# Two feed-forward products with the two parts of x side by side: one 512-column product for two of 256

## What is computed

```python
def swiglu(x, wg, wu, wd):
    return (jax.nn.silu(x @ wg) * (x @ wu)) @ wd
...
        m = jnp.einsum('bsd,df->bsf', rms_norm_2(h, mlp_norm[l]), w_mlp_in[l])
        m = jnp.square(jax.nn.relu(m))
        h = h + jnp.einsum('bsf,fd->bsd', m, w_mlp_out[l])
```

## Time and profile before

| | us |
|---|---|
| median of 3 runs | 2073.51 |
| lowest, highest | 2073.36, 2076.2 |
| the profiled execution | 2071.93 |
| its span, first to last instruction | 2069.9 |
| mean granted clock of TensorE, share of full speed | 0.976 |

### The profile page before, as it was taken

One profiled execution on the slowest core, in us unless ns is written; L12 is line 12 of the kernel. 1 busy time (PEld: TensorE's weight loads), 2 busy tenths in 40 slices (PEclk: granted clock), 3 DMA queues, 4 the chain that ended last, 5 costly groups with the idle time before them and its releaser, 6 DMA issues.

```text
span 2069.9 us, 33025 instructions
## 1 busy us (share of the span) xinstructions
PE 1932.9 (93%) x13818; PEld 1758.2 (85%) x13818; DVE 1147.3 (55%) x1219; ACT 383.9 (19%) x718; POOL 601.3 (29%) x505
## 2 busy tenths in 40 slices
PE   4899999999997878899989999889999999889999
PEld 2576777887997867799989997789999999689999
DVE  3652221325258976644575776675556676576554
ACT  1200000113122230211122122411112102432110
POOL 0111111121235611233333332133334333123333
PEclk8899999999999989999999999999999999999999
DMA  8336655321233212355544443235554434134552
GB/s 311 113 108 218 237 210 201 131 102 61 103 127 128 95 69 102 112 188 183 181 152 166 143 143 122 102 126 184 182 183 175 151 140 156 69 141 165 183 183 102
DMA packets 44913, 307.83 MB, mean 149 GB/s; under 512 B 5376, under 2 KB 5888, under 8 KB 8320
## 3 DMA queue, kind: packets, MB, share of 16 engines
q1 hardware_dynamic: 40752, 292.66, 39.8%
q10 hardware_dynamic: 4048, 13.49, 1.8%
HBM read 302.98 MB, written 3.15 MB: 148 GB/s over the span
## 4 chain that ended last, share of the span: by engine, by line
PE 78%; DVE 12%; issue 4%; POOL 2%; ACT 2%; DMA 2%; ACTq 0%; DVEq 0%; POOLq 0%
PE ps L1830 23%; PE ps L1831 22%; PE ps L1832 22%; DVE wlo L643 3%; POOL whi L570 2%; DMA ws<-in_hyc 2%; PE ps L1956 1%; PE ps L2312 1%; PE ps L1925 1%; PE ps L2219 1%; PE ps L2336 1%; DVE xlo L703 1%; PE ps L1987 1%; PE ps L2179 1%; PE ps L2289 1%
## 5 line engine op out<-in xcount | busy, mean ns | idle before, releaser
L1830 PE MATMUL ps<-xhi,whi 128*128 128x256 f32 (+1 forms) x3680 | 1121.0, 305 | 37.5 <-DVE xlo L651 21.4
L1831 PE MATMUL ps<-xlo,whi 128*128 128x256 f32 (+1 forms) x3680 | 1104.1, 300 | 0.0
L1832 PE MATMUL ps<-xhi,wlo 128*128 128x256 f32 (+1 forms) x3680 | 1103.6, 300 | 0.0
L643 DVE TENSOR_TENSOR wlo<-landing,whi 128x2048 fp32r<-128x2048 f32 x242 | 562.3, 2323 | 460.0 <-POOL whi L570 459.3
L1830 PEld LDWEIGHTS ps<-xhi,whi 128*128 128x128 f32 x3680 | 710.1, 193 | 74.2 <-issue 31.1
L1831 PEld LDWEIGHTS ps<-xlo,whi 128*128 128x128 f32 x3680 | 710.3, 193 | 22.8 <-issue 2.2
L1832 PEld LDWEIGHTS ps<-xhi,wlo 128*128 128x128 f32 x3680 | 709.6, 193 | 21.2
L569 POOL TENSOR_TENSOR whi<-landing,ones 128x128 fp32r<-128x128 f32 x242 | 124.4, 514 | 1445.1 <-PE ps L1832 1404.2
L570 POOL TENSOR_SCALAR whi<-landing 128x1920 fp32r<-128x1920 f32 x242 | 442.9, 1830 | 0.0
L881 DVE TENSOR_TENSOR big<-big,ps 128x512 f32<-128x512 f32 x22 | 15.1, 687 | 184.7 <-ACT big L1555 184.7
L1467 ACT ACTIVATE xhi<-big 128x512 fp32r (+3 forms) x66 | 45.9, 696 | 385.7 <-PE ps L1832 331.2
(11 more groups left out here) (269 smaller groups left out, 1379.3 us busy)
## 6 DMA issues: line engine op xcount, KB each, us to landing
landing<-in_stream SPq DMA_DIRECT2D x250, 1024.0 KB, 4.8
ws<-in_stream SPq DMA_DIRECT2D x28, 1024.0 KB, 4.8
spectra<-big ACTq DMA_DIRECT2D x8, 256.0 KB, 6.1
ws<-spectra ACTq DMA_DIRECT2D x2, 1024.0 KB, 4.9
ws<-in_tabs ACTq DMA_DIRECT2D x1, 1280.0 KB, 5.5
h<-in_xT ACTq DMA_DIRECT2D x1, 1024.0 KB, 15.7
ws<-in_window ACTq DMA_DIRECT2D x1, 1024.0 KB, 23.7
ws<-in_ctxT ACTq DMA_DIRECT2D x1, 1024.0 KB, 28.2
```

Of the source, the lines that this page charges most:

```text
L643: v.tensor_tensor(wlo[:, s % 2], landing[:, s], whi[:, s % 2].bitcast(F32), ALU.subtract).then_inc(lo_done, 1)
L1830: mm(out, w_hi, x_hi, start=first, stop=False, skip_group_check=True)
L1831: mm(out, w_hi, x_lo, start=False, stop=False, skip_group_check=True)
L1832: return mm(out, w_lo, x_hi, start=False, stop=last, skip_group_check=True)
```

## The change

The low part of x goes beside its high part: into columns 256 to 511 of `xhi` instead of `xlo` (lines 681 and 703 of before). A wide product of 512 columns, high weights by both parts, takes the place of two of 256; the product of low weights and high x stays. The bank of a column block then holds in its left half high by high plus low weights by high x, and in its right half high weights by low x. Each panel takes two banks in both stages, so MLP-in has two pairs in turn (banks 0 to 3) where it had four banks.

The halves are summed when the banks are read: ACT copies the right halves into `low_sums` (new, in place of value tiles not needed then), DVE adds them to the left halves into `rtmp`. Silu and the multiplication, or relu and square, work on `rtmp`. PE waits for `pair_read`, which DVE's sum raises, before it writes a pair again. In MLP-in a turn of DVE's loop is now: `low` of panel i+5, sum (`whole`) and relu of panel i+3.

```diff
-        rtmp = [W(tmpA, 2 * T), W(tmpA + 512, 2 * T)]
+        rtmp = [W(tmpA, 2, T), W(tmpA + 512, 2, T)]
+        low_sums = [W(NTABS, 2, T), W(NTABS + 512, 2, T)]
...
+        low_copied, pair_read = lsem("low_copied", N_MIN), lsem("pair_read", N_MIN)
...
-                    lo = xlo[:, j, dst0:dst0 + T]
+                    lo = xhi[:, j, T:2 * T] if n == 4 else xlo[:, j, dst0:dst0 + T]
...
-                        v.scalar_tensor_tensor(xlo[:, k, 0:T], h[:, k], gain(k), xhi[:, k, 0:T].bitcast(F32), ALU.mult,
+                        lo = xhi[:, k, T:2 * T] if j % 2 else xlo[:, k, 0:T]
+                        v.scalar_tensor_tensor(lo, h[:, k], gain(k), xhi[:, k, 0:T].bitcast(F32), ALU.mult,
...
+            def up2_stage():
                 def body(i, g, s):
                     low(g + 1, (s + 1) % SLOTS)
                     if isinstance(i, int) and i == N_UP - 1:
-                        r0 = (R_DOWN1, R_DOWN2)[which]
-                        part_low(hid_src(t)(0), r0, r0, t)
-                    dve.wait_ge(silu_done, which * KFF + i + 1)
-                    hid = hid_chunk(i, t)
-                    bank = 2 * ((s - g0) % UNROLL) + 1
-                    v.tensor_tensor(hid, hid, ps[:, bank, 0:t], ALU.mult).then_inc(hid_done, 1)
-                panel_loop(dve, g0, N_UP, body)
+                        part_low(hid_src(T)(0), R_DOWN2, R_DOWN2, T)
+                    bank = 2 * ((s - G_UP2) % UNROLL)
+                    both = rtmp[(s - G_UP2) % 2]
+                    dve.wait_ge(low_copied, i + 1)
+                    v.tensor_tensor(both, ps[:, bank:bank + 2, 0:T], low_sums[(s - G_UP2) % 2], ALU.add).then_inc(pair_read, 1)
+                    dve.wait_ge(silu_done, KFF + i + 1)
+                    hid = hid_chunk(i, T)
+                    v.tensor_tensor(hid, hid, both[:, 1], ALU.mult).then_inc(hid_done, 1)
+                panel_loop(dve, G_UP2, N_UP, body)
...
-                def relu(i, j):
-                    dve.wait_ge(panel_used, first[0] + 1 + i)
+                def whole(i, j):
+                    dve.wait_ge(low_copied, at(low_copied, l, 1, base=N_UP) + i)
                     if not isinstance(i, int) or i >= 2:
                         dve.wait_ge(m_done, at(m_done, l, -1) + i)
-                    v.scalar_tensor_tensor(rtmp[j % 2].rearrange("p (c t) -> p c t", t=T),
-                                           ps[:, j].rearrange("p (c t) -> p c t", t=T), 0.0,
-                                           rstd[:, 1].unsqueeze(1).to_broadcast([P, 2, T]), ALU.max, ALU.mult
-                                           ).then_inc(relu_done, 1)
+                    bank = 2 * (j % 2)
+                    v.tensor_tensor(rtmp[j % 2], ps[:, bank:bank + 2, 0:T], low_sums[j % 2], ALU.add).then_inc(pair_read, 1)
+                def relu(i, j):
+                    dve.wait_ge(pair_read, at(pair_read, l, 1, base=N_UP) + i)
+                    v.scalar_tensor_tensor(rtmp[j % 2], rtmp[j % 2], 0.0, rstd[:, 1].unsqueeze(1).to_broadcast([P, 2, T]),
+                                           ALU.max, ALU.mult).then_inc(relu_done, 1)
                 def low_min(i):
                     low(first[0] + i, (first[1] + i) % SLOTS)
                 low_min(1)
                 fold(2 * l + 1)
                 low_min(2)
+                whole(0, 0)
                 dve.wait_ge(inv_done, 2 * l + 2)
                 relu(0, 0)
-                low_min(3)
-                relu(1, 1)
-                relu(2, 2)
-                low_min(4)
+                for i in (1, 2):
+                    low_min(i + 2)
+                    whole(i, i)
+                    relu(i, i)
                 def relu_low(i, g, s):
-                    relu(i + 3, (s - first[1] + 3) % UNROLL)
+                    j = (s - first[1] + 3) % UNROLL
                     low(g + 5, (s + 5) % SLOTS)
+                    whole(i + 3, j)
+                    relu(i + 3, j)
                 panel_loop(dve, layer_panel(l, O_MIN), N_MIN - UNROLL, relu_low)
                 part_low(chunk_src(0)(0), rl + RO_MOUT, R_LAYER + RO_MOUT, T)
+                whole(N_MIN - 1, (N_MIN - 1) % UNROLL)
                 relu(N_MIN - 1, (N_MIN - 1) % UNROLL)
...
+            def up2_stage():
                 def body(i, g, s):
                     if isinstance(i, int) and i == N_UP - 1:
-                        act.wait_ge(hid_done, which * KFF + ROWK)
-                        first_high(hid_src(t), (R_DOWN1, R_DOWN2)[which], t, which + 1)
+                        act.wait_ge(hid_done, KFF + ROWK)
+                        first_high(hid_src(T), R_DOWN2, T, 2)
+                    bank = 2 * ((s - G_UP2) % UNROLL)
                     act.wait_ge(panel_used, g + 1)
-                    a.activation(hid_chunk(i, t), ps[:, 2 * ((s - g0) % UNROLL), 0:t], ACT.Silu).then_inc(silu_done, 1)
-                panel_loop(act, g0, N_UP, body)
+                    if not isinstance(i, int) or i >= 2:
+                        act.wait_ge(pair_read, i - 1)
+                    a.activation(low_sums[(s - G_UP2) % 2], ps[:, bank:bank + 2, T:2 * T], ACT.Identity).then_inc(low_copied, 1)
+                    act.wait_ge(pair_read, i + 1)
+                    a.activation(hid_chunk(i, T), rtmp[(s - G_UP2) % 2][:, 0], ACT.Silu).then_inc(silu_done, 1)
+                for i in range(UNROLL):
+                    body(i, G_UP2 + i, (G_UP2 + i) % UNROLL)
+                panel_loop(act, G_UP2 + UNROLL, N_UP - UNROLL, lambda i, g, s: body(i + UNROLL, g, s))
...
-                boundary_rms(2 * l + 1, step)
                 mfirst = layer_panel(l, O_MIN)
-                def square(i, g, s):
+                def copy_low(i, g, j):
+                    act.wait_ge(panel_used, g + 1)
+                    if not isinstance(i, int) or i >= 2:
+                        act.wait_ge(pair_read, at(pair_read, l, -1, base=N_UP) + i)
+                    bank = 2 * (j % 2)
+                    a.activation(low_sums[j % 2], ps[:, bank:bank + 2, T:2 * T], ACT.Identity).then_inc(low_copied, 1)
+                def square(i, j):
+                    act.wait_ge(relu_done, at(relu_done, l, 1) + i)
+                    a.activation(big[:, ds(i * 2, 2), :], rtmp[j % 2], ACT.Square).then_inc(m_done, 1)
+                for i in range(UNROLL):
+                    copy_low(i, mfirst[0] + i, i)
+                    if i == 0:
+                        boundary_rms(2 * l + 1, step)
+                    square(i, i)
+                def copy_square(i, g, s):
                     j = (s - mfirst[1]) % UNROLL
-                    act.wait_ge(relu_done, at(relu_done, l, 1) + i)
-                    a.activation(big[:, ds(i * 2, 2), :].rearrange("p c t -> p (c t)"), rtmp[j % 2], ACT.Square
-                                 ).then_inc(m_done, 1)
-                panel_loop(act, mfirst, N_MIN - UNROLL, square)
+                    copy_low(i + UNROLL, g, j)
+                    square(i + UNROLL, j)
+                panel_loop(act, layer_panel(l, O_MIN + UNROLL), N_MIN - 2 * UNROLL, copy_square)
                 for i in range(N_MIN - UNROLL, N_MIN):
                     if i == N_MIN - 1:
                         act.wait_ge(m_done, at(m_done, l, 1))
                         first_high(chunk_src(0), R_LAYER + RO_MOUT, T, at(x_free, l, 1, base=2))
-                    square(i, layer_panel(l, O_MIN + i)[0], (mfirst[1] + i) % UNROLL)
+                    copy_low(i, layer_panel(l, O_MIN + i)[0], i % UNROLL)
+                    square(i, i % UNROLL)
...
+            def wide_product(out, s, k, c, first, last):
+                w = slice(k * COLS + c * P, k * COLS + (c + 1) * P)
+                mm(out, whi[:, s % 2, w], xhi[:, k], start=first, stop=False, skip_group_check=True)
+                return mm(out[:, 0:T], wlo[:, s % 2, w], xhi[:, k, 0:T], start=False, stop=last, skip_group_check=True)
+            def wide_panel(s, bank):
+                for c in range(2):
+                    for k in range(KD):
+                        last = wide_product(ps[:, bank + c], s, k, c, k == 0, k == KD - 1)
+                return last
+            def wide_streamed(s, bank, base, order):
+                for n, k in enumerate(order):
+                    pe.wait_ge(norm_lo, base + (n + 1))
+                    for c in range(2):
+                        last = wide_product(ps[:, bank + c], s, k, c, n == 0, n == KD - 1)
+                return last
+            def wide_last(s, bank):
+                for k in range(KD):
+                    for c in range(2):
+                        last = wide_product(ps[:, bank + c], s, k, c, k == 0, k == KD - 1)
+                    if k == KD // 2 - 1:
+                        last.then_inc(x_free, 1)
                 return last
...
+            def up2_stage():
                 def one(i, g, s, reused):
-                    j = (s - g0) % UNROLL
+                    bank = 2 * ((s - G_UP2) % UNROLL)
                     pe.wait_ge(lo_done, g - (N_LEAD - 1))
```

(27 more changed lines are left out.)

10 lines of the change are left out of this document (4 added, 6 removed).

## The result

Five executions of the changed kernel took 2083.34 to 2086.72 us, median **2085.94**; five of the kernel before beside them 2072.7 to 2076.2, median 2073.51. The ratio is **1.0057** (95% interval 1.0042 to 1.0071): 12.4 us slower, where 5.7 were forecast. The profiled execution took 2086.65 us, its span 2084.9. Repeated on another chip, the same two kernels gave 2081.54 against 2072.11, ratio 1.0046 (1.0034 to 1.0058): 9.4 us.

A forecast was written before the change was run, and what follows sets the result against it. The prediction took PE, by the distance between products, to bound the kernel. Its terms, -3.7 + 0 + 6.7 + 2.7 = +5.7 us on the median 2073.51, gave 2079.2 us, range 2074.0 to 2082.5.

The forecast's parts named there:

- stretches without changed code: Stages outside second up stage, MLP-in and their hand-overs; the prediction's sum had no term for them.
- Second up stage: Wide products gain 4.3 us over 21 panels, less 0.4 and 0.2 at the two ends: -3.7 us.
- the table load: After the second up stage's panel 0, ACT's 1.28 us table load delays the chain, costing 0.4 us.
- Rival B: Weight loads set product distance; up stage falls to 5.20 us a panel, total 2072.4 us; chance 0.05.
- Rival C: Wide product gains nothing beside a narrow one; up stage stays at 5.76 us a panel, total 2083.2; chance 0.06.
- MLP-in in the steady state: Loop of POOL's copy, low part, sum and relu takes 5.75 us, taken as 5.76: 0 gained over 22 panels.
- Rival A: Relu and low part don't collide with POOL; MLP-in panels at 5.61 us, total 2074.3 us; chance 0.17.
- The stage's start: Start of MLP-in, where panel 2 waits for the sum: -0.3 to +0.3 us a layer, taken as 0.
- Hand-over: MLP-in to MLP-out: relu, square, high part and low part follow each other, +3.3 us per layer, 6.7 in all.
- Clock behind it: After PE's 3.5 us idle at MLP-out's start, granted clock falls to 0.50, costing 1.35 us per layer, +2.7.
- Rival D: Mechanism as forecast, but the clock falls in at most one layer: total 2076.5 to 2077.9 us; chance 0.15.
- the hand-over to the down stage: End of the second up stage: low part of activations ready at P + 5.43 against 5.20, costing 0.2 us.

The follow-up runs named there:

- the three profiles with the slow pitch: Three profiled executions of the changed kernel, unaltered, with product pairs at 0.3533 us in the second up stage; they took 2086.65, 2084.28 and 2085.6 us.
- the fourth: The changed kernel, unaltered, profiled on another chip with product pairs at 0.3467 us; median 2081.54 us against 2072.11 for the kernel before, ratio 1.0046.
- psum_sum: Changed kernel, but MLP-in's sum of panels 3 to 14 goes to PSUM, leaving relu one SBUF operand less; 2079.26 us against 2071.91 before, ratio 1.0033.
- mlp_only: Only MLP-in changed, second up stage left as in the kernel before; 2084.22 us, ratio 1.0057 to the kernel before.
- kept_busy: Changed kernel plus seven thrown-away products on PE between MLP-in and MLP-out; 2079.86 us against 2071.91 for the kernel before, ratio 1.0031.
- high_early: Changed kernel, but ACT makes MLP-out's first high part of activations ahead of panel 14's square; 2076.87 us against 2071.91 before, ratio 1.0017.
- grouped: Changed kernel with eight wide products, then eight narrow ones, per output half instead of alternating; 2079.26 us against 2072.13 before, ratio 1.0034.
- by_twos: Changed kernel with products ordered two wide, two narrow, and so on; 2080.71 us against 2072.11 for the kernel before, ratio 1.0037.
- up_only: Only the second up stage changed, MLP-in left as in the kernel before; 2072.62 us against 2072.13, ratio 0.9999.

## Why the prediction was wrong

The sign and the mechanisms held; what failed are terms of the sum. It (+5.7, range up to 2082.5) was too low by 7.2 us against the three profiles with the slow pitch (+12.9 from 843 on), and by 3.6 against the fourth. The largest part is a term that the prediction put at nothing without a reason, the time of the stretches without changed code (2.2 us). Then come the gain of the up stage, by the pair's cost (1.6), MLP-in's steady state (1.6), the half clock (1.0) and the hand-over (0.7). Term by term:

- **Second up stage, forecast −3.7.** Mis-sized: −2.1 with the pitch of 0.3533. The step that failed is the pair's cost, taken as 0.2273 + 0.120 from trains of one width. In a mixed train it is 0.3467 or 0.3533. With 0.3467 the stage gained 4.2, more than forecast, so the sign of this miss hangs on a draw. The added work was nearly free as argued: POOL's period after panel 0 is 6.08 us against 6.14 before, where the pitch alone would give 6.03, so little of the 0.4 was seen at which I priced the table load.
- **Rival B** (weight loads set the distance) is out: the stage runs at 5.55 to 5.65 us a panel and not 5.2. The Trainium skill (Perfetto Trace Analysis, § Identifying the Most-Contended Engine) has TensorE's headroom read from LDWEIGHTS busy rather than from matmul busy. Here it would have misled: from 878 to 1000 us PEld's share went from all of the time to 105.54 us of 122, with a third of the loads gone, and the panel shrank by 2 to 4%. **Rival C** is out too: a panel of 5.76 was not seen.
- **MLP-in in the steady state, forecast 0.** Right mechanism, mis-sized: the turn is 5.84 us, not 5.75, and costs 1.6 us in the 22 panels of both layers (1.6 to 1.8 in the four profiles). The small copy ends 0.33 behind relu (0.31 forecast), and DVE starts its low part 0.12 behind POOL's copy instead of 0.04, which is nearly all of the 0.09; why it is later I don't know. The prediction had also rounded the turn up to the 5.76 of before, and so the term to 0. The bounds, 5.61 to 5.91, held. The Trainium skill (SBUF — State Buffer, § SBUF: two separate sides) has the two engines lock each other out for a whole instruction, which would put the copy's end 0.46 behind relu: the trace agrees that each holds the other up, and has 0.33. **Rival A** is out: L571 beside relu was 0.82, not 0.46, and psum_sum shows why.
- **The stage's start, forecast 0:** 0.1 us in two layers. By layer it was −0.4 to −0.2 and +0.3 to +0.6, a little beyond the 0.3 either way that I had allowed.
- **Hand-over, forecast +6.7.** Right: the idle 3.30 and 3.39 us (3.5 forecast), the cost without clock 3.6 and 3.5 per layer (mlp_only, kept_busy), 7.1 to 7.5 in all. One link I had not seen as the cheap one to cut: ACT's order alone was 1.7 and 1.8 us of idle in the two (high_early).
- **Clock behind it, forecast +2.7.** It fell in both layers, as forecast, but for 5.1 us in layer 0 and 3.2 in layer 1: (5.1 + 3.2) x 0.44 = 3.7. (0.44 is 1 - 0.120/0.213, a 256-column product at either clock). Mis-sized by 1.0, within the bounds of 0 and 4. The prediction took 3.1 us of half clock for each layer, where its row shows 3.25; either is what layer 1 had, and layer 0's 5.1 is the miss. **Rival D**, a fall in at most one layer, did not occur in any of four profiles.
- **What had no term: stretches without changed code.** +1.5 between the up stage and MLP-in and +0.7 between the layers, 2.2 in all with the slow pitch, the largest single part of the miss (with 0.3467 it was 0.8). Behind 877 us and without the 8.3 us at the hand-overs, fp32r products of 256 columns ran at half clock for 24.4 us, before for 20.7: 3.7 x 0.44 = 1.6 of the 2.2. One whole fall of 3.2 us, at 1579.9, has no counterpart in the kernel before. 0.25 is the hand-over to the down stage, and 0.2 more of it lies in the up stage's own column; I had 0.2 for it. The rest I can't place. The forecast treated the clock as an event of one idle. But the same wait of 3.3 us was followed by a fall in layer 0 of the changed kernel and not in mlp_only, grouped and by_twos, and later stretches had other falls from program to program. up_only shows it without MLP-in's hand-over: it gave back its 2.1 us and 3 more in such stretches in its profiled execution, the slowest of eleven.

Sum with the slow pitch: −2.1 + 1.6 + 0.1 + 7.4 + 3.7 + 2.2 = 12.9.

The range was too narrow because the placement of later falls, worth up to 4 us in these runs (+0.6 to +3.8 between the layers alone), had no bound in it, and because the bounds of the terms were not added up on the same side.

## What to carry to other kernels

Before moving an instruction behind a longer one, follow who is fed by it once per stage, not only per panel: the steady state lost 1.6 us, the hand-over, one in each layer, 7.4 plus the clock. Relu with two SBUF operands, placed right before POOL's copy on DVE, closed a loop; placed early in the panel, it was held up longer (1.29 us) and cost nothing. When a gain is a few us in a program with many idles, allow for several us of clock elsewhere, and read a stage's gain from stretches of a profile rather than from the total, and look whether the profiled execution is near the median.

## What the runs showed of the hardware that I had not expected

- Alternating products of 512 and 256 columns (fp32r) have two pitches, 0.3467 and 0.3533 us a pair, 0.0067 apart, kept while PE had no idle and changed only behind one. What sets the value is open. Trains of one width showed one value in all profiles (0.228 and 0.120).
- The same idle of 3.3 to 3.4 us behind full activity was followed by half clock in eight of eight hand-overs of the changed kernel, but not in layer 0 of mlp_only, grouped and by_twos. No fall followed an idle of 1.54 and 1.64 us (high_early, two cases) or a filled one (kept_busy, two cases).
- Half clock behind such an idle lasted 2.6 to 5.3 us.
